# Rebuilding the expert stage of a hybrid RWKV-7, convolution and mixture-of-experts layer: 16 tiles, five weight buffers, an empty round without weights

## What is computed

```python
def hier_moe(h, p):
    ...
    g_p, g_idx = lax.top_k(g_prob, 1)
    ...
    e_p, e_idx = lax.top_k(jax.nn.softmax(e_sel, axis=-1), TOP_K)
    ...
    hid = jax.nn.silu(jnp.einsum('nd,edf->nef', xt, p['expert_w_gate'])) * jnp.einsum('nd,edf->nef', xt, p['expert_w_up'])
    hid = hid * combine[..., None].astype(hid.dtype)
    out = jnp.einsum('nef,efd->nd', hid, p['expert_w_down'])

    x = x + g2 * hier_moe(h, p)
...
y = rms_norm(x, final_norm_g)
```

## Time and profile before

| what | value |
| --- | --- |
| median of 3 runs | 1041.59 us (1039.92 to 1042.72) |
| profiled execution, its own time | 1038.34 us |
| its span | 1036.6 us |
| mean granted TensorE clock | 0.878 of full |
| TensorE matmul busy | 888.4 us (86%) |
| VectorE busy | 589.8 us (57%) |
| ScalarE busy | 280.1 us (27%) |
| bytes moved by DMA | 200.04 MB |

### The profile page before, as it was taken

The page is one execution under the profiler, slowest core; times in us unless marked ns, Lnnn a source line. Parts: engine busy times, 40 slices in busy tenths (PEclk is TensorE's granted clock), DMA queues, the critical chain, the costliest instruction groups (busy, mean ns, idle before and its releaser), DMA issues.

```text
span 1036.6 us, 17411 instructions
## 1 busy us (share of the span) xinstructions
PE 888.4 (86%) x6868; PEld 542.5 (52%) x6868; DVE 589.8 (57%) x1183; ACT 280.1 (27%) x510; POOL 64.5 (6%) x74
## 2 busy tenths in 40 slices
PE   3999999799988896887898899997589797898787
PEld 2466555466666575666776664454433243343332
DVE  6259999865457766777665265756733233232326
ACT  4212010321655615566422244112000000000013
POOL 0100000000000000000000000000111111111013
PEclk9899999999988658676576699998699899999999
DMA  9962553232500300302004748411899999999875
GB/s 351 357 234 96 201 210 135 94 114 80 103 2 12 23 1 12 23 2 30 4 8 57 285 174 283 174 68 64 343 355 421 418 421 421 419 420 419 351 309 225
DMA packets 75871, 200.04 MB, mean 193 GB/s; under 512 B 42061, under 2 KB 44655, under 8 KB 61583
## 3 DMA queue, kind: packets, MB, share of 16 engines
q1 hardware_dynamic: 66416, 176.41, 47.1%
q0 software_dynamic: 7456, 17.09, 4.5%
q10 hardware_dynamic: 1919, 5.44, 1.3%
HBM read 183.88 MB, written 23.40 MB: 200 GB/s over the span
## 4 chain that ended last, share of the span: by engine, by line
PE 54%; DVE 22%; DMA 12%; ACT 7%; issue 3%; SPq 2%; DVEq 0%; ACTq 0%; POOLq 0%
PE bank L596 10%; DVE arena L1051 9%; PE bank L2422 9%; DMA arena<-in_expert_w_up 7%; PE bank L1687 6%; PE bank L2443 4%; PE bank L1308 2%; ACT arena L927 2%; PE bank L1365 2%; PE bank L1295 2%; DMA arena<-winv 1%; PE bank L1368 1%; PE bank L1320 1%; PE bank L1394 1%; DVE arena L1204 1%
## 5 line engine op out<-in xcount | busy, mean ns | idle before, releaser
L596 PE MATMUL bank<-arena 128*128 128x320 f32 x704 | 206.2, 446 | 2.4 <-ACT arena L417 2.4
L596 PEld LDWEIGHTS bank<-arena 128*128 128x128 f32 x704 | 132.8, 193 | 75.6 <-issue 25.3
L2422 PE MATMUL bank<-arena 128*64 128x512 f32 (+2 forms) x496 | 119.2, 628 | 16.6 <-DMA arena<-in_expert_w_up 15.6
L1051 DVE SCALAR_TENSOR_TENSOR arena<-arena 128x655 f32<-128x655 f32 x116 | 104.7, 902 | 4.5 <-DVE arena L1051 0.2
L2422 PEld LDWEIGHTS bank<-arena 128*64 128x64 f32 (+2 forms) x496 | 44.0, 145 | 89.9 <-issue 88.8
L2511 DVE TENSOR_TENSOR arena<-arena,bank 128x256 f32<-128x256 f32 x16 | 6.8, 422 | 116.8 <-ACT arena L2469 116.8
L1687 PE MATMUL bank<-arena 128*128 128x512 f32 x160 | 70.6, 595 | 0.0
L2443 PE MATMUL bank<-arena 128*64 128x512 f32 (+2 forms) x248 | 60.4, 613 | 9.4 <-DVE arena L2514 9.4
L2469 ACT ACTIVATE arena<-bank 128x256 f32<-128x256 f32 x16 | 6.2, 385 | 197.9 <-PE bank L2422 197.9
L2178 POOL DMA_INDIRECT arena<-tokens_for_experts,arena x17 | 17.4, 1022 | 492.0 <-DVE arena L2083 465.0
L1687 PEld LDWEIGHTS bank<-arena 128*128 128x128 f32 x160 | 29.6, 189 | 34.8 <-issue 34.6
(11 more groups left out here) (368 smaller groups left out, 1332.9 us busy)
## 6 DMA issues: line engine op xcount, KB each, us to landing
arena<-in_expert_w_gate SPq DMA_DIRECT2D x33, 1024.0 KB, 16.3
arena<-in_expert_w_up SPq DMA_DIRECT2D x33, 1024.0 KB, 19.1
arena<-in_expert_w_down SPq DMA_DIRECT2D x33, 1024.0 KB, 20.5
arena<-in_ada_w SPq DMA_DIRECT2D x12, 2048.0 KB, 10.5
arena<-in_w_in SPq DMA_DIRECT2D x22, 512.0 KB, 4.1
arena<-expert_rows SPq DMA_DIRECT2D x10, 512.0 KB, 8.2
arena<-in_w_out SPq DMA_DIRECT2D x1, 4096.0 KB, 15.7
arena<-modrows SPq DMA_DIRECT2D x8, 512.0 KB, 8.5
```

The source lines that it names most:

```text
L596: mm = nc.tensor.matmul(psum[4 + 2 * (n % 2) + half][:, 0:HALF], wring[:, n % NWIN, k], hT[:, k, half * HALF:(half + 1) * HALF], start=(pa ...
L1051: chain(nc.vector.scalar_tensor_tensor(acc, src, w, acc, ALU.mult, ALU.add))
L2422: mm = nc.tensor.matmul(psum[2 + n % 2][r, :], xeT[:, n % 2, c, r], gu[:, :, c, :], start=(c == 0), stop=(c == KD - 1))
```

## The change

The tile plan has 16 tiles instead of 17. Ranks 11 and 12 and a tail of 32 places for rank 0 share one tile (64, 32 and 32 rows), ranks 13 to 28 form four quads, and three pairs remain; rank 0 now has 288 places. The routing arithmetic on DVE gets a few small operations for the tail. There are five weight buffers instead of six. The overflow round stands between tiles 11 and 12 (`OVAT` = 12) and has a turn in the ring of buffers; its weights are no longer loaded by SP but gathered by POOL, by a list of weight rows in DRAM, in which a round without rows has numbers that are out of bounds. The residual rows stay in SBUF and are neither stored nor read back, and the final gain is loaded before the experts. The last tile is an ordinary one. SP now waits for a free buffer before it reads the expert's number.

```diff
-NHOT, NPAIR, NQUAD = 6, 6, 3
-NTILE = NHOT + 1 + NPAIR + NQUAD + 1
+NHOT, TAIL = 6, 32
...
+SINGLES = [(2 + m, ((1 + m, P),)) for m in range(NHOT - 1)]
+HOT = [(0, ((0, P),)), (1, ((0, P),)), (NHOT + 1, ((11, 64), (12, 32), (0, TAIL)))]
+PAIRED = [(NHOT + 2 + m, ((a, 64), (b, 64))) for m, (a, b) in enumerate(((FIXED, 6), (7, 8), (9, 10)))]
+QUADS = [(NHOT + 5 + m, tuple((13 + m + 4 * j, 32) for j in range(4))) for m in range(4)]
...
+ROWS = ([(NTILE - 1, ((FIXED + 1, 64), (FIXED + 2, 64))), PAIRED[0], SINGLES[0], PAIRED[1], SINGLES[1], QUADS[0]] + HOT
+        + [QUADS[1], SINGLES[2], PAIRED[2], SINGLES[3], QUADS[2], SINGLES[4], QUADS[3]])
+OVAT = 12
...
-        NB = 6
+        NB = 5
...
+        for _n in range(NTILE):
+            if _n == OVAT:
+                LOADS.append("overflow")
+            LOADS += [k for k in ranks_of(_n) if k not in LOADS]
...
+        def buffer_free(t, part):
 
             sp = nc.sync
-            n = turn_of(i)
...
+            if t < NB:
+                return
+            if LOADS[t - NB] == "overflow":
+                sp.wait_ge(s_gu, OVAT + 1)
+            elif part < 2:
+                sp.wait_ge(s_gu, LAST_USE[LOADS[t - NB]] + 1)
             else:
...
+                sp.wait_ge(s_edown, LAST_USE[LOADS[t - NB]] + 1)
+
+        def experts_load(turns):
+
+            sp = nc.sync
+            number = {}
+            for parts in ((0, 1), (2,)):
+                for t in turns:
+                    k, b = LOADS[t], ebuf[t % NB]
+                    buffer_free(t, parts[0])
+                    if t < len(FIXED_EXPERTS):
+                        number[t] = FIXED_EXPERTS[k - FIXED]
+                    elif t not in number:
+                        number[t] = sp.value_load(eid[0:1, k:k + 1].bitcast(I32), min_val=0, max_val=NEXP - 1)
+                    for m in parts:
+                        name = ("expert_w_gate", "expert_w_up", "expert_w_down")[m]
+                        sp.dma_start(view(b + 2048 * m, 2048), ins[name][0, bass.ds(number[t], 1)].rearrange(
+                            "o (p c) f -> p (o c f)", p=P)).then_inc((s_egu, s_edw)[m == 2][t % NB], 16)
+
+        def load_groups():
+
+            return [[t] for t in range(NB, len(LOADS)) if t != OVTURN]
...
-                act.dma_start(x2d[i * P:(i + 1) * P, :], x2[i]).then_inc(s_h2st, 16)
...
         def pool_overflow():
             pool = nc.gpsimd
             rounds = overflow_rounds(pool)
...
+            pool.wait_ge(s_edown, LAST_USE[LOADS[OVTURN - NB]] + 1)
             with pool.Fori(0, rounds) as i:
...
+                pool.dma_start(rtab[:, 0:4].unsqueeze(1).bitcast(I32), slot_column(i + NTILE)).then_inc(s_rtab, 16)
+                pool.dma_start(rtab[:, 4:5].unsqueeze(1).bitcast(I32), weight_row(i), allow_slow_non_contiguous=True).then_inc(s_rtab, 16)
+                pool.wait_ge(s_rtab, i * 32 + 32)
...
+                for m, name in enumerate(("expert_w_gate", "expert_w_up", "expert_w_down")):
+                    pool.indirect_dma_start(out=view(buffer + 2048 * m, 2048), out_offset=None,
...
+                pool.wait_ge(s_ovdve, i * 4 + 4)
...
         def pe_overflow():
...
+            pe.wait_ge(s_eTa, OVAT + 1)
+            pe.wait_ge(s_eTd, OVAT + 1)
+            pe.wait_ge(s_eod, OVAT)
             with pe.Fori(0, rounds) as i:
...
+                pe.wait_ge(s_ovin, i * 64 + 64)
...
+            for i in range(1, BY_TENSOR):
                 second(i)
                 last(i)
+            for i in range(BY_TENSOR, TILES):
+                last(i)
...
+                if i >= BY_TENSOR:
+                    dve.wait_ge(s_fin_in[i], XT_FRONT[i] + 32)
+                    chain(nc.vector.tensor_tensor(x2[i], x2[i], yb[i], ALU.add))
```

More of the change, by code:

```diff
@@ L2006, in build @@
[L2006 to L2010 removed]
+        s_mx, s_ge, s_oh = (sem(n) for n in (
+            "gate_logits_centred", "row_buffers_cleared_then_gate_exponentials", "experts_picked"))
@@ L2673, in _constants @@
     for tile, ranks in reversed(ROWS):
-        rows = P // len(ranks)
-        for j, k in enumerate(ranks):
-            first[1, k] = rows * sum(k in r for _, r in ROWS)
-            first[0, k] = P * tile + j + len(ranks) * first[1, k]
+        for k, w, _, stride, lane in slot_places(ranks):
+            if w < P and room_of(k) > P:
+                continue
+            first[1, k] = room_of(k)
+            first[0, k] = P * tile + lane + stride * first[1, k]
             first[2, k] = P * NTILE - first[0, k]
+    first[2, 0] -= tail_shift()[0]
     own = np.zeros(P)
```

415 lines of the change are left out of this document (166 added, 249 removed).

## The result

The changed kernel takes 1080.63 us (median of 4 runs, 1077.41 to 1084.14), the kernel before 1040.76 in the same comparison (4 runs): a ratio of 1.0388, 95% interval 1.034 to 1.0436. The sign was right, the size was not: I had said 1058 and at most 1069. The profiled execution took 1079.05 us on its own, with a span of 1077.3.

What follows compares the result with a forecast made beforehand. The stage was taken as balanced: TensorE 12.7 us a tile, weight queue 8.4 us an expert. Terms summed to 277.4 against 261.7 us, +16.7 with the end; on 1038.3 that is 1055.0, plus 3.3 for the median: 1058, range 1045 to 1069.

Steps and rivals of the forecast that it cites:

- Part 8: Mixed tile 8 (64, 32, 32 columns): no extra time, up to 3.5 us if widths don't run beside each other.
- Part 5: Overflow round: TensorE waits 11 us (bounds 9 and 14) for POOL's reads and gathers, then works 19; together 30.
- The rival of the gathers that are "not empty": Overflow round: out-of-range rows cost the queue what real ones do, 3.1 MB more, +8.4 us, 1066; chance 0.1.
- Parts 4 and 7: Quads at tiles 9 and 15 wait for weights whose buffers free late, low clock included: 13.8 and 16.4 us.
- Part 6: Quad at tile 13: last expert waits for the buffer the round held; 5 us with the clock, bounds 1 and 6.
- Part 3: Up to tile 5: five buffers issue loads 10.7 us later, one expert less saves 8.4; 6 us, bounds 2 and 9.
- Part 2: First tile keeps its extra 2.7 us, waiting for tile 1's gather as before.
- Part 9: The end, from last down matmuls to end of span: 26.3 us against 25.3 before, +1.0, bounds -2 and +3.
- the two dear rivals: Overflow round: empty gathers cost like real ones (chance 0.1), or the round has rows and loads weights (0.03); each 1066.
- The tile's 12.72: Whole expert stage: a tile that waits for nothing takes 12.72 us on TensorE; 16 of them 203.5 us.

Runs made afterwards that it cites:

- e12: Changed kernel with every tile's matmuls issued width by width, so the mixed tile does its 64 wide rank first, then both 32 wide ones: 1073.2 us, ratio 1.0354.
- e1: Changed kernel with mixed tile 8 computed as four pieces of 32 columns instead of 64, 32 and 32: 1072.8 us, ratio 1.0289.
- e6: Kernel before with one pair, tile 9, computed as pieces of 64, 32 and 32 columns instead of 64 and 64: 1046.9 us, ratio 1.0051.
- e2: Changed kernel with POOL's reads and gathers for the overflow round started one tile earlier: 1064.8 us, ratio 1.0261.
- e5: Changed kernel without the overflow round's three weight gathers, TensorE waiting only for the round's rows: 1072.4 us, ratio 1.0262.
- e3: Changed kernel with loads for tile 9's last two experts and the last quad grouped, all gates and ups before the downs: 1065.5 us, ratio 1.0253.
- e7: Kernel before using five of its six weight buffers, nothing else changed: 1052.0 us, ratio 1.0104.
- e4: Changed kernel with the edits of e1, e2 and e3 together: 1050.7 us, ratio 1.010.
- e9: Changed kernel with the three edits of e4 and the overflow round moved ahead of tile 15: 1054.6 us, ratio 1.0141.
- e11: Changed kernel with the three edits of e4 and the overflow round moved ahead of tile 13: 1049.3 us, ratio 1.0089.
- e10: Kernel before, six buffers, with gates and ups issued ahead of the downs at two pairs of expert loads: 1038.5 us, ratio 1.0002.

## Why the prediction missed

**Part 8, the mixed tile**, is the largest error. I wrote "pairs and quads take the same 7.0, so 0", and for the other case up to 3.5. The earlier trace rows showed pieces of one width beside each other, never two widths, so the 0 was not in the rows. The upper bound was wrong too, half of a gate/up. Two widths that take turns are two whole passes, 7.0 more for gate/up and 3.6 for down, 10.6 (e12), and the changes add 2.7 (e1, e6). The down matmuls I had left out altogether.

**Part 5, the wait ahead of the round**: the chain was right, as e2 shows, and its landings were too short. I took 7.3 for the reads, from a round that stood at the end of the stage, and 4.5 for the empty gathers, between 2.5 and 7.2. Measured are 10.8 and 8.3 to 12.0. Counted from tile 10's start, the reads landed at 29.8 in place of 27.2, and the last gather at 45.7 in place of 36.8. The larger of two measured neighbours was the better guide, and even that was too low. I had counted each landing by itself: the reads came behind tile 14's gather, and the four gathers landed one behind the other, 2.6 us apart. The rival of the gathers that are "not empty" came out in time (8.3 us by e5, against the 8.4 it named) and not in its mechanism: no 3.1 MB were moved. The Trainium skill (DMA: Bandwidth & Descriptors, Anatomy of one DMA) has some 2 us as the fixed part of a DMA; beside a full queue the trace does not agree, four to six times that passed with nothing to move, and here the measurement decides.

**Parts 4 and 7, tiles 9 and 15**, were right in place and near in size (14.3 for 13.8; 18.2 for 16.4, just over its bound of 18), and e3 shows that it is the down load's wait that holds the next gates. **Part 6** was 2 too high. **Part 3, tile 5**: 9.0, my upper bound. I netted one expert less against the late issue. In e7, where the plan before has five buffers, a quad in that region waits 8.5. That speaks for the late issue weighing in full, but no run took the two apart. **Part 2**: the 2.7 was gone. Before, the transposes of tile 1's rows waited 1.7 us for their gather and the down behind them ran at the low clock; after, neither did. That this term is steady was an error: it is between 0 and 3.3 us in the profiles here.

**Part 9** held, 26.7 for 26.3.

**The range** was 1045 to 1069. Its upper end stood 3 above the two dear rivals, both at 1066, and below the sum of my own upper bounds (3 + 2 + 3 + 1 + 1.6 + 3.5 + 2 more than 1058.3, some 1074). Even that sum lies below the measured 1080.6, as two of the bounds were not bounds: 3.5 for part 8 and 14 for the wait of part 5. With 13 for part 8 and 20 for that wait the same sum gives 1080. That it comes out so near is in part luck, since the other terms missed by -2.7 to +3.0 and nearly cancel (+1.8).

The tile's 12.72 is 12.8 on average after, 1.9 us in 16 tiles. I took it from one single tile followed by another; the single ahead of those two took 12.82 (897.27 to 910.09), so the figure was a little low for the kernel before as well. The rest is not explained here. Nor is it explained why the four kernels with the mixed tile in pieces (e1, e4, e9, e11) started the stage at 755.0 to 759.8 and the other six of the changed kernel's line at 745.5 to 751.9. The difference stands at 330 us already, e6 with as many instructions added to the kernel before started at 749.9, and it can be chance; but it lies in the medians of e1, e4, e9 and e11, which may look up to 8 us worse than their stages.

## What to carry to other kernels

Where weights stream through a ring of buffers, look at the share of DMA window by window. Where it was 1.0, bytes decided and the order of loads gave nothing (e10). Where it had holes, the order behind the first waiting load was worth about as much (e3, 15.1 us) as a buffer (e7, 12.9). Keep pieces that share TensorE's array at one width, even if it takes more matmuls. An empty gather beside a busy queue took as long to land as one with rows (8.3 us, against 7.2 with four rows before), and several of them landed one behind the other: issue them a tile early, or don't wait for them.

## What I had not expected of the hardware

- 48 matmuls of mixed width took 15.95 us, 14.07 sorted by width, and 64 of one width for the same work 7.07.
- Gathers whose rows are all out of bounds, 0.02 MB in all, landed after 9.5 to 12.0 us while the other queue was full, 2.6 us apart though issued 1.3 apart.
- Removing three such gathers was worth 8.3 us of a wait (e5).
- With DMA at 0.00 for 20 us (963 to 983, the round) the changed kernel still starved at tile 13, 8 us later, and at tile 15: idle transfer time can't be saved up without a free buffer.
